# Differential attention in a fused decoder layer: k kept once per map with zeros, the scores as two products on all 128 channels

## The chip, the cores and the metric

The kernel runs on one core of a Trainium2 chip. The metric is the device time of one execution in microseconds (us), the median of the runs. A profile of one further execution shows what each engine did: TensorE (PE; its weight loads are shown apart as PEld), VectorE (DVE), ScalarE (ACT), GpSimd (POOL) and SyncE (SP), which issues most of the DMAs.

## The reference

One decoder layer over 256 tokens with 2048 channels: a projection, two token mixers side by side (gated DeltaNet and differential attention), gates, two further projections, a layer norm, a feed-forward part and a second layer norm. The change concerns the scores of the differential attention. It has 16 heads, each with two maps of 64 channels for q and k and 128 channels for v:

```python
def diff_attention(q, k, v, lam_params, norm_w, layer_idx):
    q = q.reshape(B, L, DA_HEADS, 2, DA_HEAD_DIM).transpose(0, 2, 3, 1, 4)
    k = k.reshape(B, L, DA_HEADS, 2, DA_HEAD_DIM).transpose(0, 2, 3, 1, 4)
    ...
    for blk in range(L // Q_BLOCK):
        start, end = blk * Q_BLOCK, (blk + 1) * Q_BLOCK
        ...
        bias = jnp.where(dist >= 0, -slopes[:, None, None] * dist, -jnp.inf)
        s = jnp.einsum('bhmqd,bhmkd->bhmqk', qb, kb).astype(jnp.float32) * scale + bias[None, :, None]
        p = jax.nn.softmax(s, axis=-1)
        p_diff = p[:, :, 0] - lam * p[:, :, 1]
        outs.append(jnp.einsum('bhqk,bhkd->bhqd', p_diff, vb.astype(jnp.float32)))
    ...
```

`Q_BLOCK` is 128, so a head has two blocks of queries: the first sees 128 keys, the second 256. With two maps that is 2 x 128 and 2 x 256 columns of scores.

## The kernel before

**The weight stream.** All weights pass through a ring of four tiles of 256 input channels by 512 output channels. SyncE loads a tile (`raw`), ScalarE rounds it (`whi`, its count is `hi_done`), VectorE takes the remainder (`wlo`, L1443, count `lo_done`), and TensorE multiplies it in `gemm_tile` with 12 products of 512 columns: two 128-channel halves, two halves of the tokens (`t`), and for each high x high, high x low and low x high. The activations are the stationary operand, the weights the moving one, the sums stand in the PSUM banks `pg`. ScalarE and VectorE work three tiles ahead of TensorE (`AHEAD`).

**Bodies and slots.** A `body` is 32 weight tiles, in four groups of eight; each tile is a slot `s` of 0 to 31. Every engine runs the same body, and at given slots it does a step of the token mixers besides its share of the weight stream. The order on each engine is the order in which the code is written; semaphores (`N[...]`) tie the engines together. After four bodies of the DeltaNet part comes a body that projects the first four heads' q, k and v of the attention (`N_DA`) and ends the DeltaNet part, then four bodies in each of which `da_mix` does the attention of four heads (`HB`), while the body's weights project the next four heads' q, k and v; the last of the four is `N_GB`.

**The attention of a head.** At slots 0, 5, 10 and 15 (`HEAD_SLOTS`) TensorE makes one head's scores, from `qT` (stationary) and `kT` (moving), both f32 with the channels on the partitions: map 0 is on partitions 0 to 63, map 1 on 64 to 127. For each block of queries `t` and each map `m` there is one product on 64 partitions, of 128 columns for `t` = 0 and 256 for `t` = 1; map 0 goes to bank `B[1]`, map 1 to `B[2]`. VectorE waits for `pe_s`, adds the ALiBi bias in one instruction for each map (384 columns), and takes the maxima; ScalarE makes the exponentials; VectorE normalizes and subtracts at `s0 + 2`; GpSimd moves p out to DRAM and back in pieces to transpose it (`turn_p`); at slots 10, 15, 20 and 25 (`PV_SLOTS`) TensorE multiplies p with v, three products of 128 columns on all 128 partitions.

**Where kT comes from.** For the first four heads VectorE transposes k in 16 blocks of 32 partitions in slots 16 to 23 of the body `N_DA` (`da_turns`, L1854). For the others ScalarE sends k through DRAM, and VectorE turns it in one instruction of 1024 elements a partition at slot 29 (`qk_rows`, L1840); q likewise at slot 21.

**Memory.** `act_b` takes the attention's result, high and low half, 16 heads of 256 tokens each. Until then its room holds the DeltaNet part's buffers (`cT`, `decm`, `T`, `Pm` and others).

Of the kernel before, what the change touches and what calls it, by code (L numbers as in the profile page):

```python
# [22 lines left out]
P = 128  # L23
# [5 lines left out]
HB = 4  # L29
# [75 lines left out]
def build(nc, xT, xrow, weights, w_ab, consts, early, params, lam_in, ln_in, out):  # L105
    ctx = ExitStack()

    def sb(name, shape, dt=F32):
        return ctx.enter_context(nc.sbuf_tensor(name, shape, dt))
# [4 lines left out]
    with ctx:  # L114
# [25 lines left out]
        stage = tmp("stage", [P, 4, 8, SB])  # L140
        oT = tmp("oT", [P, 4, 8, SB])
        dn.close()
        act_b = sb("act_b", [P, 2, KC, SEQ], F32R)
        gates = sb("gates", [P, 2, TOK, D])
        y = gates[:, 0]
# [40 lines left out]
        def c(name):  # L186
            a, b = CONST[name]
            return cst[:, a:b]
# [68 lines left out]
        def landed(buf):  # L257
            return flat(buf[:, :, :]).rearrange("p (a q x) -> p a q x", a=4, x=SB)

        def last_four(jj):  # L260
            return isinstance(jj, int) and jj == NB - 1

# [42 lines left out]
        def end_at(s):  # L305
# [25 lines left out]
        x_hi = sem("x_hi")  # L331
        x_lo = sem("x_lo")
        once = """pe_passed pe_ab pe_abT act_ab2 dve_ab2 act_abT dve_two pe_sc0 act_pro dve_pro dve_sc0 act_tot dve_lam act_lam
            dve_lnT dve_x1 pe_x1T x1f act_x1T dve_x1T pe_y act_beta act_gc pe_gT act_gT act_var dve_var act_root act_sig act_xn pro_chain ln_chain""".split()

        counted = """pe_conv dve_raw dve_conv act_silu dve_cw act_tap
            dve_g act_past act_decay pe_ktok act_sqk dve_ktail pe_kk dve_at dve_t act_tt dve_a8 pool_t8 dve_x pe_x pe_p dve_p pe_t
# [136 lines left out]
        def _(pe):  # L474
# [223 lines left out]
            def da_mix(j, s):  # L698
                for h, s0 in enumerate(HEAD_SLOTS):
                    if s == PV_SLOTS[h]:  # L700
                        pe.wait_ge(N["dve_pT"], 1 + HB * j + h + 1)
                        pe.wait_ge(N["dve_oh2"], 1 + HB * j + max(h - 1, 0))
                        pe.wait_ge(N["dve_oT"], 1 + 2 * NB)
                        o = B[3 if h % 2 == 0 else 0]
                        mm(o[:, 0:P], pT[:, 0:P], vda[:, 0, h * P:(h + 1) * P])
                        mm(o[:, P:2 * P], pT[:, P:2 * P], vda[:, 0, h * P:(h + 1) * P], True, False)
                        mm(o[:, P:2 * P], pT[:, 2 * P:3 * P], vda[:, 1, h * P:(h + 1) * P], False, True
                           ).then_inc(N["pe_pv"], 1)
                for h, s0 in enumerate(HEAD_SLOTS):
                    if s == s0:  # L710
                        pe.wait_ge(N["dve_qkT"], 1 + 2)
                        pe.wait_ge(N["dve_qkS"], 1 + 2 * j)
                        pe.wait_ge(N["dve_s1"], 1 + HB * j + h)
                        pe.wait_ge(N["dve_oT"], 1 + 2 * NB)
                        for t in range(TOK):
                            for m in range(2):
                                a = slice(m * CH, (m + 1) * CH)
                                last = mm(B[1 + m][:, t * P:t * P + (t + 1) * P],
                                          qT[a, h, t * P:(t + 1) * P], kT[a, h, 0:(t + 1) * P])
                        last.then_inc(N["pe_s"], 1)  # L720

            def turn_rows(cnt, n):
# [650 lines left out]
        def _(pool):  # L1373
# [23 lines left out]
            for j in range(NB + 1):  # L1397
                if j > 0:
                    pool.wait_ge(N["dve_qs"], 1 + j)
                    root(d_("rs"), d_("qs")).then_inc(N["pool_rs"], 1)  # L1400
                if j < NB:
                    pool.wait_ge(N["dve_ss"], 1 + j + 1)
                    ch(root(d_("rk"), d_("ss")))
                    G.tensor_tensor(d_("rinv"), d_("rk"), d_("ss"), ALU.mult).then_inc(N["pool_rinv"], 1)
                    pool.wait_ge(N["dve_a8"], 1 + j + 1)
                    for k in range(EB - 1):
                        col, row, part, rest = below(k)
                        ch(G.tensor_tensor(part, col, row, ALU.mult))  # L1408
                        last = G.tensor_tensor(rest, rest, part, ALU.subtract)  # L1409
                        if k < EB - 2:  # L1410
                            ch(last)
                    last.then_inc(N["pool_t8"], 1)
                    for i in range(2):
                        pool.wait_ge(c_kept, 16 * (2 * j + i + 1))
                        pool.wait_ge(N["dve_raw"], 1 + 2 * j + i)
                        blocks_in(turn_c, moved, c_full)
                    pool.wait_ge(v_kept, 16 * (j + 1))
                    blocks_in(turn_v, vtok, v_full)
            def os_root(i):

                pool.wait_ge(N["dve_os"], 1 + i + 1)
                root(sm[:, 48:50], sm[:, 42:44]).then_inc(N["pool_os"], 1)
# [16 lines left out]
        def _(dve):  # L1439
# [316 lines left out]
            def da_mix(j, s, ch):  # L1756
# [4 lines left out]
                for h, s0 in enumerate(HEAD_SLOTS):  # L1761
                    if s == s0:
                        dve.wait_ge(N["pe_s"], 1 + HB * j + h + 1)
                        dve.wait_ge(N["dve_pd"], 1 + HB * j + h)
                        for m in range(2):
                            ins = stt(pr[:, m, :], c("negdist"), sm[:, 44 + h:45 + h], B[1 + m][:, 0:3 * P],
                                      ALU.mult, ALU.add)
                        ins.then_inc(N["dve_s1"], 1)
                        dve.wait_ge(N["dve_s1"], 1 + HB * j + h + 1)
                        V.tensor_reduce(sm[:, 24:26], pr[:, :, 0:P], X, ALU.max)  # L1770
                        ch(V.tensor_reduce(sm[:, 26:28], pr[:, :, P:3 * P], X, ALU.max))
                        ts(sm[:, 28:32], sm[:, 24:28], -1.0, ALU.mult).then_inc(N["dve_mx"], 1)
# [61 lines left out]
            def qk_rows(j, s):  # L1834

                if s in DA_ROWS:
                    which = DA_ROWS.index(s)
                    dve.wait_ge(q_full, 64 * (2 * j + which - 1))
                    dve.wait_ge(N["pe_s"], 1 + HB * j)
                    V.transpose((qT, kT)[which][:, :, :].rearrange("p h (t a x) -> p a (h t) x", t=TOK, x=SB),  # L1840
                                gate_b(0).rearrange("p (a q i) -> p a q i", a=4, i=SB)).then_inc(N["dve_qkS"], 1)

            def da_turns(s):

                for which, slots in enumerate(DA_TURN_FIRST):
                    if s not in slots:
                        continue
                    at = sum(n for k, n in slots.items() if k < s)
                    if at == 0:
                        dve.wait_ge(evac[which], 2 * NB + 1)  # L1850
                    out = blocks_out((qT, kT)[which][:, :, :])
                    for i in range(at, at + slots[s]):
                        a, b = divmod(i, 4)
                        ins = V.transpose(out[b * SB:(b + 1) * SB, :, :, a, :], blocks_in[a * SB:(a + 1) * SB, :, :, b, :])  # L1854
                    if i == 15:
                        ins.then_inc(N["dve_qkT"], 1)
# [385 lines left out]
```

## Time and profile before

| | |
|---|---|
| time, median of 3 runs | 1903.24 us (1902.1 to 1903.43) |
| the profiled execution's own time | 1903.3 us |
| its span, first to last instruction | 1901.4 us |
| TensorE busy | 1885.8 us, 99% |
| VectorE busy | 1314.3 us, 69% |
| ScalarE busy | 918.5 us, 48% |
| GpSimd busy | 216.5 us, 11% |
| granted TensorE clock, mean | 0.998 |

The busy time of an engine is the union of its records. A record of TensorE lasts from its start until its last result is out, so records that follow each other overlap, and the starts, not the durations, show what one costs. An f32 product stands in the trace as two records, a product of the weight stream as one, though both are printed as f32. Idle time of an engine that isn't the bottleneck costs nothing.

### The profile page before, as it was taken

Reading aid. Unit: us, or ns where it says so; the run is one execution under the profiler, and the core shown is the slowest. Engines: PE = TensorE matmul, PEld = TensorE weight load, DVE = VectorE, ACT = ScalarE, POOL = GpSimd, SP = SyncE. Lnnn points to the kernel's source line nnn. Section 1 sums busy time; section 2 is a strip of 40 time slices with the busy share of each in tenths; the row PEclk is TensorE's granted clock in tenths of the full one; section 3 lists DMA queues with packets and bytes.
Section 4 is the critical chain, followed back from the end, with each engine's and each line's share of the span. In section 5 each row is a group of like instructions: output and inputs, shape, how many; then the busy total and the mean of one; then the engine's idle time right before and its main releaser. Section 6 shows DMA issues by size and latency. Waiting matters only on the chain.

```text
span 1901.4 us, 30042 instructions
## 1 busy us (share of the span) xinstructions
PE 1885.8 (99%) x9703; PEld 1554.5 (82%) x9703; DVE 1314.3 (69%) x1816; ACT 918.5 (48%) x1270; POOL 216.5 (11%) x480
## 2 busy tenths in 40 slices
PE   9999999999999999999999999999999999999997
PEld 7888888878888888888888887888888888888886
DVE  7878788787766767676577657667775466655656
ACT  5656565554454545456444437444443444443442
POOL 0303031131024232323000000000000000000000
PEclk9999999999999999999999999999999999999999
DMA  7666657574557676766656675555656556655555
GB/s 271 209 193 211 211 190 222 173 241 155 194 190 244 213 248 206 247 211 210 209 189 198 222 248 173 194 193 190 196 192 196 190 191 197 197 191 196 189 190 175
DMA packets 115091, 387.61 MB, mean 204 GB/s; under 512 B 14193, under 2 KB 21169, under 8 KB 114865
## 3 DMA queue, kind: packets, MB, share of 16 engines
q1 hardware_dynamic: 97904, 351.65, 56.5%
q10 hardware_dynamic: 11712, 22.04, 3.6%
q0 software_dynamic: 5376, 12.59, 2.4%
q8 instruction: 64, 1.05, 0.2%
q14 instruction: 35, 0.28, 0.1%
HBM read 367.86 MB, written 18.37 MB: 203 GB/s over the span
## 4 chain that ended last, share of the span: by engine, by line
PE 92%; DVE 3%; issue 1%; POOL 1%; DMA 1%; ACT 1%; SPq 0%; DVEq 0%; ACTq 0%; POOLq 0%
PE pg L476 87%; PE B L476 4%; DVE gates L1451 1%; DVE cT L1451 1%; POOL Tc L1408 1%; DMA qT<-turn_c 1%; ACT whi L854 1%; DVE wlo L1443 0%; DMA raw<-in_weights 0%; POOL Tc L1409 0%; POOL qT L1394 0%; PE B L576 0%; PE B L595 0%; PE B L689 0%; DVE Pm L1443 0%
## 5 line engine op out<-in xcount | busy, mean ns | idle before, releaser
L1443 DVE TENSOR_TENSOR wlo<-raw,whi 128x1024 fp32r<-128x1024 f32 (+1 forms) x640 | 778.9, 1219 | 470.2 <-ACT whi L854 452.8
L854 ACT ACTIVATE whi<-raw 128x1024 fp32r<-128x1024 f32 (+1 forms) x640 | 673.7, 1057 | 731.9 <-PE pg L476 712.5
L476 PE MATMUL pg<-whi,act_x 128*128 128x512 f32 x2960 | 938.6, 393 | 1.7 <-ACT whi L854 1.7
L476 PEld LDWEIGHTS pg<-whi,act_x 128*128 128x128 f32 x2960 | 555.5, 188 | 124.8 <-issue 7.9
L476 PE MATMUL pg<-wlo,act_x 128*128 128x512 f32 x1480 | 574.5, 389 | 0.0
L476 PE MATMUL pg<-whi,act_a 128*128 128x512 f32 x1632 | 504.8, 389 | 0.2 <-DVE act_a L1443 0.2
L476 PEld LDWEIGHTS pg<-whi,act_a 128*128 128x128 f32 x1632 | 306.3, 188 | 64.3 <-DVE act_a L1443 0.8
L476 PEld LDWEIGHTS pg<-wlo,act_x 128*128 128x128 f32 x1480 | 278.1, 188 | 54.6
L476 PE MATMUL pg<-wlo,act_a 128*128 128x512 f32 x816 | 317.4, 389 | 0.0
L476 PEld LDWEIGHTS pg<-wlo,act_a 128*128 128x128 f32 x816 | 153.2, 188 | 31.7
L476 PE MATMUL pg<-whi,act_b 128*128 128x512 f32 x512 | 158.5, 389 | 0.0
L476 PEld LDWEIGHTS pg<-whi,act_b 128*128 128x128 f32 x512 | 96.1, 188 | 20.0
L476 PE MATMUL pg<-wlo,act_b 128*128 128x512 f32 x256 | 99.6, 389 | 0.0
L1884 DVE STREAM_TRANSPOSE soft<-hraw 32x256 f32<-32x256 f32 x208 | 90.6, 436 | 3.8
L476 PEld LDWEIGHTS pg<-wlo,act_b 128*128 128x128 f32 x256 | 48.0, 188 | 10.0
L1383 POOL TENSOR_TENSOR half<-dsm 128x8 f32<-128x8 f32 x24 | 13.2, 550 | 264.9 <-DVE dsm L1448 263.6
L1451 DVE SCALAR_TENSOR_TENSOR cT<-vda,cw,cT 128x255 f32<-128x255 f32 (+2 forms) x96 | 41.9, 478 | 1.1
L1156 ACT ACTIVATE soft<-soft,sm 128x128 f32<-128x128 f32 (+1 forms) x64 | 28.4, 445 | 27.8 <-DVE sm L1447 27.7
L1385 POOL TENSOR_SCALAR half<-half 128x2 f32<-128x2 f32 (+1 forms) x72 | 32.2, 448 | 6.3
L1451 DVE SCALAR_TENSOR_TENSOR soft<-cst,sm,B 128x384 f32<-128x384 f32 x32 | 18.2, 611 | 21.0 <-PE B L476 20.3
L1394 POOL DMA_DIRECT2D gates<-turn_p x48 | 26.2, 552 | 38.2 <-DMA turn_p<-gates 38.2
L993 ACT ACTIVATE cT<-cT 128x1024 f32<-128x1024 f32 x12 | 12.7, 1062 | 23.6 <-DVE cT L1451 23.6
(259 smaller groups left out, 1100.5 us busy)
## 6 DMA issues: line engine op xcount, KB each, us to landing
raw<-in_weights SPq DMA_DIRECT2D x646, 512.0 KB, 4.2
turn_c<-hraw ACTq DMA_DIRECT2D x8, 512.0 KB, 3.9
qT<-turn_c POOLq DMA_DIRECT2D x32, 128.0 KB, 3.2
turn_q<-hraw ACTq DMA_DIRECT2D x6, 512.0 KB, 3.8
gates<-turn_q ACTq DMA_DIRECT2D x24, 128.0 KB, 4.8
turn_p<-gates POOLq DMA_DIRECT2D x12, 192.0 KB, 3.7
gates<-turn_p POOLq DMA_DIRECT2D x48, 48.0 KB, 3.9
decm<-sums_out ACTq DMA_DIRECT2D x4, 512.0 KB, 3.7
```

The source lines that it names most:

```text
L476: return nc.tensor.matmul(o, l, r, start=start, stop=stop)
L854: return nc.scalar.activation(o, i, ACT.Copy, scale=scale)
L993: nc.scalar.activation(cT[:, kind], cT[:, kind], ACT.Silu).then_inc(N["act_silu"], 1)
L1156: last = nc.scalar.activation(pr[:, m, a:b], pr[:, m, a:b], ACT.Exp, bias=sm[:, 28 + i:29 + i], accum_out=sm[:, 32 + i:33 + i])
L1383: ch(G.tensor_tensor(a, o, o, ALU.mult))
L1385: ch(G.tensor_scalar(a, a, -0.5, 1.5, ALU.mult, ALU.add))
L1394: pool.dma_start(dst[b * SB:(b + 1) * SB], scratch[:, :, b].rearrange("a x (q i) -> x a q i", i=SB)).then_inc(full, 16)
L1408: ch(G.tensor_tensor(part, col, row, ALU.mult))
L1443: return V.tensor_tensor(o, a, b, op)
L1451: return V.scalar_tensor_tensor(out=o, in0=a, scalar=s, in1=b, op0=op0, op1=op1)
L1884: ins = V.transpose(blocks_out(turned)[b * SB:(b + 1) * SB, :, :, a, :], blocks_in[a * SB:(a + 1) * SB, :, :, b, :])
```

## The change

- k is no longer kept in `kT` but in `k_span`, once for each map: map 0's copy has its own 64 channels on partitions 0 to 63 and zeros on 64 to 127, map 1's the other way round. Product and sum over all 128 partitions then give one map's scores, since the other map's channels of q meet zeros.
- `k_span` lies in the part of `act_b` that belongs to the last four heads' results, which are written after the last scores; its two halves are 4096 elements apart.
- GpSimd writes the zeros once, after its last work for the DeltaNet part and ahead of the first move of p; TensorE waits for that (`pool_zero`) in front of each head's scores.
- A head's scores are two products, one for each block of queries: the moving operand is map 0's and map 1's keys, one behind the other, 256 columns for `t` = 0 into `B[1]` and 512 for `t` = 1 into `B[2]`.
- VectorE adds the bias in one instruction for each block of queries (256 and 512 columns).
- `qk_rows` turns k in two instructions of 64 partitions, `da_turns` writes its 16 blocks to the map that they belong to.

```diff
--- before.py
+++ after.py
@@ -140,6 +140,10 @@
         stage = tmp("stage", [P, 4, 8, SB])
         oT = tmp("oT", [P, 4, 8, SB])
         dn.close()
+        da = ExitStack()
+        da.enter_context(nc.sbuf_tensor("da_below", [P, (KC - HB) * SEQ], F32))
+        k_span = da.enter_context(nc.sbuf_tensor("k_span", [P, 2, KC * SEQ], F32))
+        da.close()
         act_b = sb("act_b", [P, 2, KC, SEQ], F32R)
         gates = sb("gates", [P, 2, TOK, D])
         y = gates[:, 0]
@@ -257,6 +261,12 @@
         def landed(buf):
             return flat(buf[:, :, :]).rearrange("p (a q x) -> p a q x", a=4, x=SB)
 
+        k_maps = [k_span[:, m, 0:HB * SEQ].rearrange("p (h s) -> p h s", h=HB) for m in range(2)]
+        MAPS = [slice(0, CH), slice(CH, P)]
+
+        def both_maps(h, n):
+            return k_span[:, :, h * SEQ:h * SEQ + n]
+
         def last_four(jj):
             return isinstance(jj, int) and jj == NB - 1
 
@@ -331,7 +341,7 @@
         x_hi = sem("x_hi")
         x_lo = sem("x_lo")
         once = """pe_passed pe_ab pe_abT act_ab2 dve_ab2 act_abT dve_two pe_sc0 act_pro dve_pro dve_sc0 act_tot dve_lam act_lam
-            dve_lnT dve_x1 pe_x1T x1f act_x1T dve_x1T pe_y act_beta act_gc pe_gT act_gT act_var dve_var act_root act_sig act_xn pro_chain ln_chain""".split()
+            dve_lnT pool_zero dve_x1 pe_x1T x1f act_x1T dve_x1T pe_y act_beta act_gc pe_gT act_gT act_var dve_var act_root act_sig act_xn pro_chain ln_chain""".split()
 
         counted = """pe_conv dve_raw dve_conv act_silu dve_cw act_tap
             dve_g act_past act_decay pe_ktok act_sqk dve_ktail pe_kk dve_at dve_t act_tt dve_a8 pool_t8 dve_x pe_x pe_p dve_p pe_t
@@ -712,11 +722,11 @@
                         pe.wait_ge(N["dve_qkS"], 1 + 2 * j)
                         pe.wait_ge(N["dve_s1"], 1 + HB * j + h)
                         pe.wait_ge(N["dve_oT"], 1 + 2 * NB)
+                        pe.wait_ge(N["pool_zero"], 1)
                         for t in range(TOK):
-                            for m in range(2):
-                                a = slice(m * CH, (m + 1) * CH)
-                                last = mm(B[1 + m][:, t * P:t * P + (t + 1) * P],
-                                          qT[a, h, t * P:(t + 1) * P], kT[a, h, 0:(t + 1) * P])
+                            n = (t + 1) * P
+                            last = mm(B[1 + t][:, 0:2 * n].rearrange("p (m s) -> p m s", m=2),
+                                      qT[:, h, t * P:(t + 1) * P], both_maps(h, n))
                         last.then_inc(N["pe_s"], 1)
 
             def turn_rows(cnt, n):
@@ -1416,6 +1426,13 @@
                         blocks_in(turn_c, moved, c_full)
                     pool.wait_ge(v_kept, 16 * (j + 1))
                     blocks_in(turn_v, vtok, v_full)
+            pool.wait_ge(N["act_x21"], 1 + NB)
+            pool.wait_ge(N["dve_qk"], 1 + 2 * NB)
+            pool.wait_ge(N["pool_rs"], 1 + NB)
+            ch(G.memset(k_maps[0][MAPS[1]], 0.0))
+            G.memset(k_maps[1][MAPS[0]], 0.0).then_inc(N["pool_zero"], 1)
+            pool.wait_ge(N["pool_zero"], 1)
+
             def os_root(i):
 
                 pool.wait_ge(N["dve_os"], 1 + i + 1)
@@ -1762,9 +1779,9 @@
                     if s == s0:
                         dve.wait_ge(N["pe_s"], 1 + HB * j + h + 1)
                         dve.wait_ge(N["dve_pd"], 1 + HB * j + h)
-                        for m in range(2):
-                            ins = stt(pr[:, m, :], c("negdist"), sm[:, 44 + h:45 + h], B[1 + m][:, 0:3 * P],
-                                      ALU.mult, ALU.add)
+                        for t, (a, b) in enumerate([(0, P), (P, 3 * P)]):
+                            ins = stt(pr[:, :, a:b], rep(c("negdist")[:, a:b], 2), sm[:, 44 + h:45 + h],
+                                      B[1 + t][:, 0:2 * (b - a)].rearrange("p (m s) -> p m s", m=2), ALU.mult, ALU.add)
                         ins.then_inc(N["dve_s1"], 1)
                         dve.wait_ge(N["dve_s1"], 1 + HB * j + h + 1)
                         V.tensor_reduce(sm[:, 24:26], pr[:, :, 0:P], X, ALU.max)
@@ -1837,8 +1854,16 @@
                     which = DA_ROWS.index(s)
                     dve.wait_ge(q_full, 64 * (2 * j + which - 1))
                     dve.wait_ge(N["pe_s"], 1 + HB * j)
-                    V.transpose((qT, kT)[which][:, :, :].rearrange("p h (t a x) -> p a (h t) x", t=TOK, x=SB),
-                                gate_b(0).rearrange("p (a q i) -> p a q i", a=4, i=SB)).then_inc(N["dve_qkS"], 1)
+                    rows = gate_b(0).rearrange("p (a q i) -> p a q i", a=4, i=SB)
+
+                    def by_token(dst):
+                        return dst.rearrange("p h (t a x) -> p a (h t) x", t=TOK, x=SB)
+                    if which == 0:
+                        last = V.transpose(by_token(qT[:, :, :]), rows)
+                    else:
+                        for m in range(2):
+                            last = V.transpose(by_token(k_maps[m][MAPS[m]]), rows[MAPS[m]])
+                    last.then_inc(N["dve_qkS"], 1)
 
             def da_turns(s):
 
@@ -1848,9 +1873,9 @@
                     at = sum(n for k, n in slots.items() if k < s)
                     if at == 0:
                         dve.wait_ge(evac[which], 2 * NB + 1)
-                    out = blocks_out((qT, kT)[which][:, :, :])
                     for i in range(at, at + slots[s]):
                         a, b = divmod(i, 4)
+                        out = blocks_out(qT[:, :, :] if which == 0 else k_maps[b // 2])
                         ins = V.transpose(out[b * SB:(b + 1) * SB, :, :, a, :], blocks_in[a * SB:(a + 1) * SB, :, :, b, :])
                     if i == 15:
                         ins.then_inc(N["dve_qkT"], 1)
```

TensorE's order in the second body of the attention, at the slot where p times v of the first head is followed by the third head's scores: `B1` and `B2` are the banks of the scores, `B3` that of p times v, `pg` those of the weight stream. Before:

```order
L476 MATMUL pg11<-wlo,act_x 128x512
L476 MATMUL pg11<-whi,act_x 128x512
L476 MATMUL B3<-vda,soft 128x128 x3
L713 REGISTER_ALU
L476 MATMUL B1<-kT,qT 128x128
L476 MATMUL B2<-kT,qT 128x128
L476 MATMUL B1<-kT,qT 128x256
L476 MATMUL B2<-kT,qT 128x256
L501 REGISTER_ALU
L476 MATMUL pg10<-whi,act_x 128x512
```

After:

```order
L486 MATMUL pg11<-wlo,act_x 128x512
L486 MATMUL pg11<-whi,act_x 128x512
L486 MATMUL B3<-vda,soft 128x128 x3
L723 REGISTER_ALU
L486 MATMUL B1<-k_span,qT 128x256
L486 MATMUL B2<-k_span,qT 128x512
L511 REGISTER_ALU
L486 MATMUL pg10<-whi,act_x 128x512
```

Nothing moved past anything; the four products of the scores are two, at the same place.

VectorE's order from the k turn at slot 29 of the first body of the attention to the scores' bias in the next one (`wlo` is the weight split, `sm` holds slopes and maxima). Before:

```order
L1451 SCALAR_TENSOR_TENSOR gates<-gates,par 128x256
L1840 STREAM_TRANSPOSE kT<-gates 128x4x8x32
L1443 TENSOR_TENSOR wlo<-raw,whi 128x1024 x2
...
L1759 COPY sm<-cst 128x4
L357 ISA
L1763 REGISTER_ALU
L1451 SCALAR_TENSOR_TENSOR soft<-cst,sm,B 128x384 x2
L1770 TENSOR_REDUCE sm<-soft 128x2
```

After:

```order
L1468 SCALAR_TENSOR_TENSOR gates<-gates,par 128x256
L1865 STREAM_TRANSPOSE k_span<-gates 64x4x8x32 x2
L1460 TENSOR_TENSOR wlo<-raw,whi 128x1024 x2
...
L1776 COPY sm<-cst 128x4
L367 ISA
L1780 REGISTER_ALU
L1468 SCALAR_TENSOR_TENSOR soft<-cst,sm,B 128x2x128
L1468 SCALAR_TENSOR_TENSOR soft<-cst,sm,B 128x2x256
L1787 TENSOR_REDUCE sm<-soft 128x2
```

One transpose of k became two of half the partitions, ahead of the next weight split; the two instructions of the bias have other shapes.

## Rows read from the trace of the kernel before

**Rows 1.** The page, busy us of each engine (share of the span) xinstructions.
```profile
PE 1885.8 (99%) x9703; PEld 1554.5 (82%) x9703; DVE 1314.3 (69%) x1816; ACT 918.5 (48%) x1270; POOL 216.5 (11%) x480
...
PEclk9999999999999999999999999999999999999999
```

**Rows 2.** TensorE's waits, the largest: waited for, us in all, times, longest.
```profile
PE pg L476 <- ACT whi L854: 1.7, 3, 0.9
```

**Rows 3.** TensorE's timeline: start us, us from first start to last end, instruction xcount.
```profile
530.12 0.39 PE L476 MATMUL pg<-whi,act_x 128*128 128x512 f32 x1
530.44 0.93 PE L476 MATMUL B<-kT,qT 64*128 64x128 f32 x8
531.29 0.50 PE L476 MATMUL pg<-whi,act_x 128*128 128x512 f32 x1
...
543.22 0.39 PE L476 MATMUL pg<-wlo,act_x 128*128 128x512 f32 x1
...
543.90 0.39 PE L476 MATMUL pg<-wlo,act_x 128*128 128x512 f32 x1
...
544.81 0.39 PE L476 MATMUL pg<-whi,act_x 128*128 128x512 f32 x1
...
559.49 0.40 PE L476 MATMUL pg<-whi,act_x 128*128 128x512 f32 x1
...
574.83 0.40 PE L476 MATMUL pg<-whi,act_x 128*128 128x512 f32 x1
...
590.16 0.40 PE L476 MATMUL pg<-whi,act_x 128*128 128x512 f32 x1
590.39 0.83 PE L476 MATMUL B<-vda,soft 128*128 128x128 f32 x6
...
604.48 0.40 PE L476 MATMUL pg<-whi,act_x 128*128 128x512 f32 x1
...
636.43 0.39 PE L476 MATMUL pg<-whi,act_x 128*128 128x512 f32 x1
```

**Rows 4.** The same timeline in four narrow windows inside the first score block.
```profile
530.44 0.38 PE L476 MATMUL B<-kT,qT 64*128 64x128 f32 x2
...
530.65 0.50 PE L476 MATMUL B<-kT,qT 64*128 64x128 f32 x4
...
530.76 0.39 PE L476 MATMUL B<-kT,qT 64*128 64x256 f32 x2
...
530.98 0.38 PE L476 MATMUL B<-kT,qT 64*128 64x256 f32 x2
```

**Rows 5.** Groups by form, 480 to 900 us: xcount | busy us, mean ns | idle before.
```profile
L476 PE MATMUL B<-vda,soft 128*128 128x128 f32 x96 | 13.3, 275 | 0.0
L476 PEld LDWEIGHTS B<-vda,soft 128*128 128x128 f32 x96 | 13.2, 191 | 1.3
```

**Rows 6.** The same view, VectorE's bias step.
```profile
L1451 DVE SCALAR_TENSOR_TENSOR soft<-cst,sm,B 128x384 f32<-128x384 f32 x32 | 18.2, 611 | 21.0 <-PE B L476 20.3 <-DVE sm L1759 0.7
```

**Rows 7.** VectorE's timeline, at a k turn and behind a bias step; idle time in brackets.
```profile
616.87 1.24 DVE L1840 STREAM_TRANSPOSE kT<-gates 128x1024 f32<-128x1024 f32 x1
618.04 1.18 DVE L1443 TENSOR_TENSOR wlo<-raw,whi 128x1024 fp32r<-128x1024 f32 x1
620.38 1.23 DVE L1443 TENSOR_TENSOR wlo<-raw,whi 128x1024 fp32r<-128x1024 f32 x1 [1.16 <-ACT whi L854]
...
632.11 1.23 DVE L1443 TENSOR_TENSOR wlo<-raw,whi 128x1024 fp32r<-128x1024 f32 x1 [1.73 <-ACT whi L854]
```

**Rows 8.** GpSimd's timeline, the first move of p.
```profile
540.13 0.61 POOL L1429 DMA_DIRECT2D turn_p<-gates  x1 [68.37 <-DVE gates L1451]
```

**Rows 9.** Timelines of TensorE and its weight loads, the warm-up products at the start.
```profile
3.34 1.06 PE L476 MATMUL B<-TTf 128*128 128x512 f32 x1
...
4.19 1.06 PE L476 MATMUL B<-TTf 128*128 128x512 f32 x1
...
3.34 0.34 PEld L476 LDWEIGHTS B<-TTf 128*128 128x128 f32 x1 [0.52 <-issue]
```

## The prediction

> **What bounds the kernel now.** I read the busy shares first: TensorE is busy in 1885.8 of 1901.4 us [rows 1]. Then the view of who waited for whom, for TensorE: its largest entry is 1.7 us, for ScalarE's rounding of the weights [rows 2]. So no other engine holds TensorE anywhere for long, and a change in the length of TensorE's own work goes to the end one to one, as long as what feeds it keeps its lead. The attention scores are TensorE's work. What a block of them costs has to be read as time added between two weight products, because a record's own duration contains its run through the array and overlaps its neighbour's.
>
> **What the score block costs now.** The timeline of TensorE gives the last weight product ahead of slots 0, 5, 10, 15, 20 and 25 of a body: 530.12, 544.81, 559.49, 574.83, 590.16 and 604.48 [rows 3]. Between two of them stand five weight tiles, 60 products, and what the attention puts in. The step of a weight product is (543.90 - 543.22)/3 = 0.2267 us [rows 3], so 60 take 13.60. What is left is
> - slots 0 and 5, scores alone: 14.69 - 13.60 = 1.09 and 14.68 - 13.60 = 1.08, mean 1.085;
> - slots 10 and 15, a p·v block and then scores: 15.34 and 15.33, so 1.74 and 1.73, mean 1.735;
> - slot 20 (and 25), p·v alone: 14.32 - 13.60 = 0.72.
> There are four such bodies, so 8 score blocks stand alone and 8 behind a p·v.
>
> Inside a block [rows 4]: an f32 product is two records, one for each pass over its columns. The eight records start in four pairs, at 530.44, 530.65, 530.76 and 530.98: map 0 on channels 0 to 63 and map 1 on channels 64 to 127 start together and stream side by side. So the two maps' 128 + 256 columns cost once: the columns of a pair step 0.11 (128) and 0.22 (256). Four pairs of columns are 2 x 0.107 + 2 x 0.213 = 0.64 us. The other 0.445 us of 1.085 is the changeover: the first record starts 0.32 behind the weight product instead of 0.23, the second pair 0.21 behind the first where 128 columns need 0.11 (its weights weren't loaded ahead), and the weight product comes back at 531.29, 0.31 behind the last pair's start where 256 columns need 0.21 [rows 3, 4]; the rest is the first weight products behind the block, which load late.
>
> The Trainium skill's "TensorEngine Tiling (Array Packing)", section Key Properties, states both halves: tiles work independently, and changing the tiling mode drains the engine. The trace agrees with both, with the pairs and with the 0.09 and 0.10 us at the two ends. The second half speaks for this change: taken alone it would make the kernel 16 x 0.19 = 3.0 us faster; the first half speaks against it, and by the rows it is the larger.
>
> **What it costs after.** The order of the changed program shows on TensorE, in place of four products on 64 channels, two on all 128: one of 256 columns into bank 1 and one of 512 into bank 2. With 128 channels in use nothing streams beside them. Records: 2 of 256 and 2 of 512 columns.
> - Price of a pass. The p·v block is the nearest row: whole-array f32 products back to back. Its six records take 0.83 in the timeline, the last of them 0.275 [rows 3, 5], so the step is (0.83 - 0.275)/5 = 0.111 for 128 columns, which is 0.1067 (two cycles a column at 2.4 GHz; the granted clock is at 9 tenths or more in every slice [rows 1]) and 0.005. Low end: columns alone, 12 x 0.1067 = 1.28. Taken: 1.28 and 0.005 for each of four records, 1.30. High end: the step of weight products, 0.2267 where 512 single columns are 0.2133, is 6% over its columns; so 1.36. I take 1.30, because p·v is the same data type in the same mode.
> - Price of the way in and out. p·v alone adds 0.72, of which 6 x 0.1116 = 0.67 are steps; 0.05 stay for coming and going without a change of mode.
> - Scores alone: 1.30 + 0.05 = 1.35 against 1.085, +0.265, 8 times: 2.12 us.
> - Scores behind p·v: 0.67 + 1.30 + 0.05 = 2.02 against 1.735, +0.285, 8 times: 2.28 us.
> - Sum +4.40 us. With the low end 8 x 0.245 + 8 x 0.265 = 4.08, with the high end 8 x 0.325 + 8 x 0.345 = 5.36.
>
> **The parts beside it.**
> - VectorE's bias step: two instructions of 384 elements, 0.611 each [rows 6], become one of 256 and one of 512, the same 768 elements; the nearest is no change. It starts 0.27 later. The smallest lead I found for weights is behind such a step: the split that starts at 632.11 and takes 1.23 feeds the tile that starts at 636.43 [rows 3, 7], so 3.09 us are left. 0.27 fit. Cost 0; uncovered, 0.27 per head.
> - The k turn between bodies: one transpose of 1024 elements, 1.24 [rows 7], becomes two on 64 partitions each. Since the elements of a partition set the time, I take +1.24, three times (bodies 2 to 4). It pushes the split behind it from 618.04 to 619.28, its end to 620.5; the next split stood idle 1.16 until 620.38 [rows 7]. So it is taken up within a slot. Below nothing it can't go, for the elements don't shrink. The first body's 16 block transposes are the same number as before.
> - GpSimd's zeroing: two fills of 64 x 1024, once. No fill of that size stands in the trace. GpSimd is idle for 68.37 us before 540.13, so from 471.77 on [rows 8]; what is queued behind the fills is the first move of p at 540.13, and TensorE asks at 530.4. Anything from nothing to 58.6 us for the two fills is hidden; at 60 us it would cost 1.4. I take 0. The waits ahead of the fills are for steps of the DeltaNet part, which are over by then.
> - TensorE's new wait is for a semaphore that rises once, long before; its sequencer runs ahead of the array as it does at p·v, where the weights are loaded under the product before. Queued behind it are the scores and all later weight tiles. Cost 0.
>
> Span 1901.4 + 4.4 = 1905.8. The profiled execution's own time is 1903.3, 1.9 over its span and 0.06 over the median, so the same sum is made on the median: 1903.24 + 4.40 = **1907.6 us**.
>
> **Rivals.**
> - A, faster: an f32 pass over whole columns is as cheap as a weight product's. The rows tempt to it, both are printed 128x512 f32, and the weight product steps 0.2267. Then the scores take 2 x 0.113 + 2 x 0.227 = 0.68; alone 0.73 (-0.355), behind p·v 1.40 (-0.335): -5.5 us, 1897.7. It decides from a 512-column step of 0.34 downwards (3 steps of that are 1.30 - 0.275). Against it: p·v, 0.111 for 128 columns, and the pair of 256 at 0.22. Chance 0.04.
> - B, smaller loss: part of a record's step is a fixed price, so that half as many, longer records save. If 0.025 of p·v's 0.1116 were fixed, 256 columns would take 0.198 and 512 0.371: 1.14 in all, alone +0.105, behind p·v +0.125, +1.8 us, 1905.1. Against it: 0.11 and 0.22 for 128 and 256 leave nothing fixed [rows 4]. The Trainium skill's tiling page, section Instruction Overhead, speaks of about 60 cycles for each matmul on trn2, which is the 0.025 at 2.4 GHz; the trace doesn't agree, with 0.005. Chance 0.05.
> - C, larger loss: the 512-column pass is slow. The only whole-array f32 passes of 512 in the trace step 0.85 (3.34 to 4.19) [rows 9]. Then 2 x 0.42 more per head, 13.4 us, 1921.1. Against it: weight loads there take 0.34, and 0.19 at p·v [rows 5, 9], so this stretch ran at the lower clock level, though it stands ahead of the first clock record. For it: the moving operand is now in two pieces far apart, and no row has such a product. Chance 0.03.
> - D: VectorE loses its lead and the three turns come through: 3.7 us more, 1911.3. Chance 0.03.
>
> **How the numbers follow.** The forecast has 0.85. About 0.2% of this kernel, 3.8 us, is what a measurement can tell from no change, and the forecast lies just beyond it: its bounds are 4.1 to 5.4, while the shown runs of the kernel before lie between 1.14 below and 0.19 above their median. So 0.13 of the 0.85 goes to "same". Slower: 0.72 + C + D = 0.78. Same: 0.13 + B = 0.18. Faster: A, 0.04. Range: 1903.24 + 4.08 - 1.14 = 1906.2 to 1903.24 + 5.36 + 0.67 (half the spread of the runs) = 1909.3; that leaves out the four rivals, 0.15 in all.
>
> **What would show it.** In the profile after: four records of the scores per head, steps of 0.22 (256 columns) and 0.43 (512); the first one 0.23 behind the weight product, not 0.32; the weight product right behind the last; 14.95 us between the weight products ahead of slots 0 and 5, and 15.62 for slots 10 and 15, each in place of 14.69 and 15.33; TensorE's waits as small as before. I am wrong if the 512-column step is far from 0.43 (A, B, C), if TensorE waits for VectorE's splits (D), or if the way in still costs a changeover, which would add up to 0.4 us per head.

## The result: 0.22% slower, and the profile after

The changed kernel takes 1907.16 us (median of 17 runs, 1906.08 to 1909.21), the kernel before in the same comparison 1902.45 us (17 runs, 1901.8 to 1903.84). The ratio is 1.0022, with a 95% interval of 1.0015 to 1.0029: 4.7 us more, and between 2.9 and 5.5 by the interval. The forecast was +4.4 us. The profiled span is 1905.2 us.

The page of the changed kernel, engine busy times (the line that answers to [rows 1]), and the largest waits of TensorE (that of [rows 2]; who waited for whom: us in total, times, longest):

```profile
PE 1889.6 (99%) x9639; PEld 1558.3 (82%) x9639; DVE 1317.3 (69%) x1819; ACT 918.3 (48%) x1270; POOL 217.3 (11%) x482
```

```profile
PE B L486 <- DVE TTf L1490: 1.5, 1, 1.5
PE pg L486 <- ACT whi L864: 1.4, 2, 0.8
```

The first of them stands in the view of the kernel before as well, just below the line of [rows 2]:

```profile
PE B L476 <- DVE TTf L1473: 1.5, 1, 1.5
```

TensorE has 3.8 us more to do and 64 records less, four for each head. Nothing new holds it: no entry names VectorE's weight splits (`wlo`), GpSimd or the zeroing, and from 529 to 890 us, over the attention's four bodies, the view of TensorE's waits is empty in both kernels. VectorE has 3.0 us more: the three k turns are 3.7 us longer, and a little went elsewhere.

TensorE's timeline of the changed kernel at the first scores and at the last weight product ahead of slots 0, 5, 10, 15, 20 and of the next body's slot 0 (start, us from the first start to the last end, instruction, count):

```profile
529.65 0.40 PE L486 MATMUL pg<-whi,act_x 128*128 128x512 f32 x1
529.88 1.46 PE L486 MATMUL B<-k_span,qT 128*128 128x256 f32 x4
530.78 0.79 PE L486 MATMUL pg<-whi,act_x 128*128 128x512 f32 x1
531.41 0.40 PE L486 MATMUL pg<-wlo,act_x 128*128 128x512 f32 x1
...
544.59 0.40 PE L486 MATMUL pg<-whi,act_x 128*128 128x512 f32 x1
...
559.53 0.40 PE L486 MATMUL pg<-whi,act_x 128*128 128x512 f32 x1
...
575.11 0.40 PE L486 MATMUL pg<-whi,act_x 128*128 128x512 f32 x1
...
590.69 0.40 PE L486 MATMUL pg<-whi,act_x 128*128 128x512 f32 x1
...
624.77 0.40 PE L486 MATMUL pg<-whi,act_x 128*128 128x512 f32 x1
```

Against [rows 3]: 14.94 us twice in place of 14.69 and 14.68, 15.58 twice in place of 15.34 and 15.33. So a head's scores cost 0.25 us more, alone and behind p·v alike, and the way from slot 0 to the next body's slot 0 is 95.12 us. In the kernel before it is 94.12 (530.12 to the row below), so 1.00 us a body and 4.0 us for the four bodies:

```profile
624.24 0.39 PE L476 MATMUL pg<-whi,act_x 128*128 128x512 f32 x1
```

The difference of the two profiled spans is 3.8; the 0.2 that are missing lie outside the attention: the changed kernel came to slot 0 at 529.65 and not at 530.12, 0.5 earlier, in a part that the change doesn't touch, and lost 0.3 again behind the attention.

The same timeline in three narrow windows inside the first block, for the steps ([rows 4] of before):

```profile
530.11 0.81 PE L486 MATMUL B<-k_span,qT 128*128 128x256 f32 x2
...
530.32 1.02 PE L486 MATMUL B<-k_span,qT 128*128 128x512 f32 x2
...
530.75 0.59 PE L486 MATMUL B<-k_span,qT 128*128 128x512 f32 x1
```

With 529.88 for the first record the starts are 529.88, 530.11, 530.32 and 530.75: 0.44 for the two records of 256 columns, so 0.22 each, and 0.43 for the first of 512. The first record stands 0.23 behind the weight product, where it was 0.32. The record of the weight product that follows starts at 530.78, only 0.03 behind the last one, but that start is not its price: the record after it comes at 531.41, 0.66 behind 530.75, which is the 0.43 of the last scores and one weight step of 0.23. There is no changeover left, and no two records of the scores start together.

### The profile page after: what moved, and what is told of

It reads as the page before. It is cut to its first block, busy times and chain, and to the rows that moved or that the text cites. A ratio compares the mean times of both kernels' runs of the same rounds, so it can differ in the third digit from the quotient of the medians.

```text
span 1905.2 us, 29921 instructions
## 1 busy us (share of the span) xinstructions
PE 1889.6 (99%) x9639; PEld 1558.3 (82%) x9639; DVE 1317.3 (69%) x1819; ACT 918.3 (48%) x1270; POOL 217.3 (11%) x482
## 4 chain that ended last, share of the span: by engine, by line
PE 95%; DVE 2%; issue 1%; ACT 1%; DMA 1%; POOL 0%; SPq 0%; DVEq 0%; ACTq 0%; POOLq 0%
PE pg L486 90%; PE B L486 5%; DVE gates L1468 1%; DMA raw<-in_weights 0%; ACT whi L864 0%; DMA qT<-turn_c 0%; DVE wlo L1460 0%; DVE cT L1468 0%; POOL Tc L1418 0%; PE B L586 0%; PE B L699 0%; PE B L605 0%; POOL Tc L1419 0%; DVE act_b L1460 0%; ACT gates L1287 0%
## 5 line engine op out<-in xcount | busy, mean ns | idle before, releaser
L1468 DVE SCALAR_TENSOR_TENSOR soft<-cst,sm,B 128x256 f32<-128x256 f32 (+1 forms) x32 | 18.2, 611 | 26.6 <-PE B L486 25.4
```

The lines of the kernel that those rows point to most:

```text
L1468: return V.scalar_tensor_tensor(out=o, in0=a, scalar=s, in1=b, op0=op0, op1=op1)
```

## The experiments

All are compared by the same two places of TensorE's timeline: the last weight product ahead of slot 0, and the one ahead of slot 5 (or of slot 0 in the next body). From 528 to 890 us no run shows a wait of TensorE, so the time between two such places depends on TensorE's own work alone.

### What stands around the products: x1_kept

The changed kernel with the old products on the new storage:

```diff
                         for t in range(TOK):
-                            n = (t + 1) * P
-                            last = mm(B[1 + t][:, 0:2 * n].rearrange("p (m s) -> p m s", m=2),
-                                      qT[:, h, t * P:(t + 1) * P], both_maps(h, n))
+                            for m in range(2):
+                                a = slice(m * CH, (m + 1) * CH)
+                                last = mm(B[1 + m][:, t * P:t * P + (t + 1) * P],
+                                          qT[a, h, t * P:(t + 1) * P], k_maps[m][a, h, 0:(t + 1) * P])
...
-                        for t, (a, b) in enumerate([(0, P), (P, 3 * P)]):
-                            ins = stt(pr[:, :, a:b], rep(c("negdist")[:, a:b], 2), sm[:, 44 + h:45 + h],
-                                      B[1 + t][:, 0:2 * (b - a)].rearrange("p (m s) -> p m s", m=2), ALU.mult, ALU.add)
+                        for m in range(2):
+                            ins = stt(pr[:, m, :], c("negdist"), sm[:, 44 + h:45 + h], B[1 + m][:, 0:3 * P],
+                                      ALU.mult, ALU.add)
```

> The changed kernel with its scores put back: k stays kept once per map with the zeros, the two-part k turn, GpSimd's zeroing and TensorE's wait for it stay, but the scores are again four products on 64 partitions with a bank for each map, and the bias is added per map. My theory (the loss is TensorE's columns, which no longer run two maps side by side): the score blocks cost what they did, 14.69 and 15.33 us between the weight products ahead of slots 0 and 5 and of slots 10 and 15, and the time is that of the kernel before, within 0.2 us in the span. Rival (the loss comes from what stands around the products: the longer k turn, the zeroing, the wait): the time stays near the changed kernel's, 3.8 us over the kernel before.

Measured: 1903.48 us against 1902.94, ratio 1.0003 (0.9994 to 1.0012), span 1900.3. TensorE's timeline, ahead of slots 0 and 5 and of the next body's slot 0:

```profile
528.75 0.39 PE L486 MATMUL pg<-whi,act_x 128*128 128x512 f32 x1
...
543.44 0.39 PE L486 MATMUL pg<-whi,act_x 128*128 128x512 f32 x1
...
622.87 0.39 PE L486 MATMUL pg<-whi,act_x 128*128 128x512 f32 x1
```

14.69 and 94.12 us, as in the kernel before. So storage, zeros, k turn and the new wait cost nothing, and the whole 1.00 us a body is in the form of the products and of the bias step, which this run puts back too. (The bias step's new form stays in x4_one_map_128 below, where TensorE waits for nothing either.) The span is 1.1 less than the kernel before's and not within 0.2 as expected; the difference arises ahead of the attention, 528.75 against 530.12. A comparison of single spans of this kernel is good to about that much, while the stretch between two places comes out alike in all four bodies.

### The pairing: x3_one_map_64, x6_same_rows, x2_map_major

Three edits of the kernel before. In the first, map 1 is left out:

```diff
-                            for m in range(2):
+                            for m in range(1):
...
-                            ins = stt(pr[:, m, :], c("negdist"), sm[:, 44 + h:45 + h], B[1 + m][:, 0:3 * P],
+                            ins = stt(pr[:, m, :], c("negdist"), sm[:, 44 + h:45 + h], B[1][:, 0:3 * P],
```

> The kernel before with map 1's score products left out (two products a head on 64 partitions; VectorE reads map 0's scores for both maps, so the second map is not computed). Theory: map 1 ran under map 0, so leaving out half of the score work gives back almost nothing on TensorE: 14.65 to 14.69 us between the weight products ahead of slots 0 and 5, time within 0.5 us of the kernel before. Rival (every record pays its own columns): half of the columns gone is 0.32 us a head or more, at least 5 us less.

Measured: 1902.81 us, ratio 0.9997 (0.9988 to 1.0006). Its score block, and the way to slot 5:

```profile
528.74 0.39 PE L476 MATMUL pg<-whi,act_x 128*128 128x512 f32 x1
529.05 0.92 PE L476 MATMUL B<-kT,qT 64*128 64x128 f32 x4
529.90 0.50 PE L476 MATMUL pg<-whi,act_x 128*128 128x512 f32 x1
...
543.42 0.39 PE L476 MATMUL pg<-whi,act_x 128*128 128x512 f32 x1
```

Four records where there were eight, and 14.68 us where there were 14.69. In the kernel before, map 1 costs TensorE next to nothing.

In the second, both maps' products are put on partitions 0 to 63; map 1's own channels are left out, and map 0's are used twice:

```diff
-                                a = slice(m * CH, (m + 1) * CH)
+                                a = slice(0, CH)
```

> The kernel before with map 1's products made from map 0's channels, so that all four products of a head are on partitions 0 to 63 (map 1 is not computed from its own channels, its scores are those of map 0). Still two changeovers, but no second group of rows to stream beside. The exchanged loops didn't separate the maps, since the records of the two halves paired up again; this does. Theory: the columns add up, 1.28 us in place of 0.64: +0.64 for each of 16 heads, +10.2 us over the kernel before, so the mode with 64 channels is by itself slower than the changed kernel (by 5.5 to 6 us) and owes its lead to the pairing alone. Rival (64 channels are quicker for another reason than the pairing): less than 5 us over the kernel before.

Measured: 1912.65 us, ratio 1.0054 (1.0041 to 1.0068), span 1910.7, so +10.3 us by the ratio.

```profile
529.21 0.39 PE L476 MATMUL pg<-whi,act_x 128*128 128x512 f32 x1
529.53 1.57 PE L476 MATMUL B<-kT,qT 64*128 64x128 f32 x8
531.03 0.50 PE L476 MATMUL pg<-whi,act_x 128*128 128x512 f32 x1
...
544.54 0.39 PE L476 MATMUL pg<-whi,act_x 128*128 128x512 f32 x1
```

The same eight records now last 1.57 and not 0.93 [rows 3], the way is 15.33: +0.64 a head, which is the 0.64 us of columns that ran beside the others. The smaller products owe their lead over the changed kernel to the pairing alone; one after the other on 64 partitions they are 0.39 us a head slower than it.

The third was meant to separate the maps in another way, by order:

```diff
-                        for t in range(TOK):
-                            for m in range(2):
+                        for m in range(2):
+                            for t in range(TOK):
```

> The kernel before with the two loops around its four score products exchanged: both blocks of queries of map 0 first, then both of map 1, same products, same partitions, same banks. In the kernel before the partner of each record on the other 64 partitions stands next to it; here only the last record of map 0 and the first of map 1 are neighbours. Theory: the array keeps the order of records, so only that pair overlaps: columns 0.107 + 0.107 + 0.213 + 0.213 + 0.213 + 0.213 = 1.07 us a head in place of 0.64, so +0.43 for 16 heads, +6.9 us over the kernel before and about 3 us over the changed one, since both changeovers stay as well. Rival (the near-simultaneous starts are only how the records look and the two maps do not run side by side): no difference, 0 us.

Measured: 1902.8 us, ratio 0.9999 (0.999 to 1.0008). Neither theory as I had written it: the time is the rival's, and the rival's reason is refuted by the two runs above. The order of the program as it was built is map 0's two products, then map 1's:

```
L476 MATMUL B1<-kT,qT 128x128
L476 MATMUL B1<-kT,qT 128x256
L476 MATMUL B2<-kT,qT 128x128
L476 MATMUL B2<-kT,qT 128x256
```

and TensorE's timeline in narrow windows inside the block is

```profile
529.00 0.39 PE L476 MATMUL B<-kT,qT 64*128 64x128 f32 x2
...
529.22 0.50 PE L476 MATMUL B<-kT,qT 64*128 64x128 f32 x4
...
529.33 0.39 PE L476 MATMUL B<-kT,qT 64*128 64x256 f32 x2
...
529.55 0.39 PE L476 MATMUL B<-kT,qT 64*128 64x256 f32 x2
```

Two records of 128 columns start together at 529.00, two at 529.22 (the line there counts the next pair in, x4), two of 256 columns at 529.33 and two at 529.55. In the program map 0's 256-column records stand ahead of all of map 1's, yet all four records of 128 columns, map 1's two among them, start ahead of any record of 256. The trace doesn't say which record of a pair is whose. As x6_same_rows shows that records on the same rows don't share their time, each pair must be one record of each map; so each half of the rows works through its own records, and the halves don't wait for each other. Loops exchanged or not, the pairs form again.

### The changeover: x4_one_map_128, x5_two_heads

The changed kernel with map 0 alone, so with as long a stream of columns as the pairs of the kernel before, but on the whole array:

```diff
-                            last = mm(B[1 + t][:, 0:2 * n].rearrange("p (m s) -> p m s", m=2),
-                                      qT[:, h, t * P:(t + 1) * P], both_maps(h, n))
+                            last = mm(B[1 + t][:, 0:n], qT[:, h, t * P:(t + 1) * P], k_maps[0][:, h, 0:n])
...
-                                      B[1 + t][:, 0:2 * (b - a)].rearrange("p (m s) -> p m s", m=2), ALU.mult, ALU.add)
+                                      rep(B[1 + t][:, 0:b - a], 2), ALU.mult, ALU.add)
```

> The changed kernel with only map 0's scores: two products on all 128 partitions of 128 and 256 columns, VectorE reads them for both maps, so the second map is not computed. It has the same length of columns in time as the pairs of the kernel before (0.64 us a head), but no change of mode, so it prices the changeover. Theory: per head 0.64 + 0.02 + 0.05 = 0.71 alone and 1.34 with p times v in front of it, against 1.085 and 1.735: -0.375 x 8 - 0.395 x 8 = -6.2 us against the kernel before, and 0.64 x 16 = 10.2 us less than the changed kernel. Rival (a record has a large fixed price, or the 512-column form is what is slow): against the changed kernel clearly less than 10.2 us is saved, or clearly more.

Measured: 1897.4 us, ratio 0.9971 (0.996 to 0.9982), span 1895.0.

```profile
528.99 0.40 PE L486 MATMUL pg<-whi,act_x 128*128 128x512 f32 x1
529.22 0.82 PE L486 MATMUL B<-k_span,qT 128*128 128x128 f32 x4
529.69 0.58 PE L486 MATMUL pg<-whi,act_x 128*128 128x512 f32 x1
...
543.29 0.40 PE L486 MATMUL pg<-whi,act_x 128*128 128x512 f32 x1
...
621.59 0.40 PE L486 MATMUL pg<-whi,act_x 128*128 128x512 f32 x1
```

14.30 us to slot 5, so 0.70 for the block, and 92.60 for the body: 1.52 less than the kernel before, 0.38 a head. That is what going to 64 rows and back costs. Against the changed kernel it is 2.52 a body, 0.63 a head: the columns of the second map. The change is the sum of the two: -0.38 and +0.63, +0.25. For the four bodies the two are 6.1 and 10.1 us, where 6.2 and 10.2 were expected.

Where the 0.38 lies shows in the starts. This run's second and last record and the second weight product behind the block:

```profile
529.33 0.49 PE L486 MATMUL B<-k_span,qT 128*128 128x128 f32 x2
...
529.66 0.38 PE L486 MATMUL B<-k_span,qT 128*128 128x256 f32 x1
...
530.11 0.40 PE L486 MATMUL pg<-wlo,act_x 128*128 128x512 f32 x1
```

and that weight product in the kernel before:

```profile
531.63 0.39 PE L476 MATMUL pg<-wlo,act_x 128*128 128x512 f32 x1
```

On the way in the second record starts 0.34 behind the weight product ahead of the block (529.33 - 528.99); in the kernel before the second pair starts 0.53 behind it (530.65 - 530.12 [rows 3, 4]). On the way out the second weight product starts 0.45 behind the last record here and 0.65 behind the last pair there (531.63 - 530.98). That is 0.19 and 0.20. The first record behind each change of mode shows only half of that (0.09 and 0.10, as the prediction has it), the second one the rest. The weight loads go with it: in the kernel before they begin together with the products that they are for, behind a gap, at 530.44 and at 531.29:

```profile
530.44 0.52 PEld L476 LDWEIGHTS B<-kT,qT 64*128 64x128 f32 x8 [0.35 <-issue]
531.29 0.19 PEld L476 LDWEIGHTS pg<-whi,act_x 128*128 128x128 f32 x1 [0.33 <-issue]
```

In the changed kernel the first load of the scores runs under the weight product that starts at 529.65, 0.23 ahead of its own product:

```profile
529.65 0.85 PEld L486 LDWEIGHTS B<-k_span,qT 128*128 128x128 f32 x4
```

If a block costs 0.38 us for the changeover, heads in one block should share it. The kernel before with the second head's scores moved to slot 0:

```diff
+SCORE_SLOTS = [0, 0, 10, 15]
...
+        def score_bank(h, m):
+            return B[3 * m] if h == 1 else B[1 + m]
...
-                for h, s0 in enumerate(HEAD_SLOTS):
+                for h, s0 in enumerate(SCORE_SLOTS):
                     if s == s0:
+                        if h == 1:
+                            pe.wait_ge(N["dve_oh2"], 1 + HB * j)
...
-                        pe.wait_ge(N["dve_s1"], 1 + HB * j + h)
+                        pe.wait_ge(N["dve_s1"], 1 + HB * j + (h if h > 1 else 0))
```

with `score_bank(h, m)` for `B[1 + m]` in the products and in the bias step.

> The kernel before with the scores of the first two heads of a body made in one block at slot 0 (the second head's into the two banks of p times v, which are free then), instead of at slots 0 and 5; VectorE takes the second head at slot 5 as before. The products are the same, but a body has one changeover less. Theory (a changeover in and out costs about 0.42 us a block, columns 0.64): 4 x 0.42 = 1.7 us less than the kernel before, so about 1901.2 us and 5.5 us less than the changed kernel. Rival (what a block costs beyond its columns belongs to each head or record, not to the change of mode): no change.

Measured: 1901.05 us, ratio 0.9991 (0.9982 to 1.0).

```profile
529.33 0.39 PE L480 MATMUL pg<-whi,act_x 128*128 128x512 f32 x1
529.65 1.58 PE L480 MATMUL B<-kT,qT 64*128 64x128 f32 x16
...
558.26 0.40 PE L480 MATMUL pg<-whi,act_x 128*128 128x512 f32 x1
...
623.01 0.39 PE L480 MATMUL pg<-whi,act_x 128*128 128x512 f32 x1
```

Sixteen records take 1.58 where eight take 0.93: the second head adds 0.65, its columns and next to nothing. The body is 93.68 us, 0.44 less than before, 1.76 for the four. That is more than x4's 0.38, because a block less also saves the 0.06 that x4's block costs over its columns (0.70 - 0.64) without any change of mode. The interval of the times only just reaches no change; the timeline is clear.

### Two changeovers less: x7_two_pairs

The same for both pairs of heads. The banks have room: a head takes 384 of 512 columns in `B[1]` and `B[2]`, p·v 256 in `B[0]` and `B[3]`. The second head of a pair goes into what is left:

```diff
-HEAD_SLOTS = [0, 5, 10, 15]
+HEAD_SLOTS = [0, 5, 10, 14]
+SCORE_SLOTS = [0, 0, 10, 10]
...
+        def score_at(h, m, a, b):
+            if h % 2 == 0:
+                return B[1 + m][:, a:b]
+            if b <= P:
+                return B[1 + m][:, 3 * P + a:3 * P + b]
+            return B[3 * m][:, P + a:P + b]
```

TensorE makes the scores ahead of p·v at slot 10, its later p·v wait for the fourth head's bias step, and VectorE waits for both heads of a pair.

> As the run with two heads in one block at slot 0, and the third and fourth head also in one block, at slot 10 ahead of the first p times v: the second head of a pair goes into the columns of the four banks that are otherwise unused, and the fourth head's bias step moves from slot 15 to slot 14. Two changeovers less in each body. Theory: 8 x 0.42 = 3.4 us less than the kernel before, about 1899.6 us; a few tenths may go to p times v standing alone at slot 15. If TensorE has to wait for the fourth head's bias step at slot 15, the gain is smaller and shows as a wait for VectorE. Rival (no price for the changeover): no change.

Measured: 1899.59 us against 1902.84, ratio 0.9985 (0.9976 to 0.9994), span 1898.3.

```profile
530.64 0.39 PE L484 MATMUL pg<-whi,act_x 128*128 128x512 f32 x1
...
559.89 1.58 PE L484 MATMUL B<-kT,qT 64*128 64x128 f32 x16
...
623.99 0.39 PE L484 MATMUL pg<-whi,act_x 128*128 128x512 f32 x1
```

The body is 93.35 us (530.64 to 623.99), 0.77 less than before and 1.77 less than in the changed kernel: 3.1 us for the four bodies, where 3.4 were expected. Part of what is missing is that p·v at slot 15 no longer shares its way in and out with scores; no run takes that apart. It is faster than the kernel before with an interval that leaves out no change, and faster than the changed kernel by 7.1 us of the bodies.

## Why the prediction was right

- **The bound.** TensorE's own work goes to the end one to one: +4.0 us in the attention's bodies, +4.7 in the medians with an interval of 2.9 to 5.5. How near the number came is in part luck. The bodies' 4.0 lie just under the low end of the forecast's sum, 4.08, and the 0.7 more that the medians show is within their interval and has no cause that a run shows. The sum also started from 1903.24, the median of three runs, which is 0.8 above that of the 17; so the time came out 0.4 below the forecast although the measured change is 0.3 above it.
- **What the block cost.** 0.64 of columns for two maps and the rest changeover. Shown: taking map 1 away changes 0.01 us of 14.69, putting it on the same rows adds 0.64.
- **The changeover's size.** The 0.19 us that I read at the two ends (0.09 and 0.10) are half of it. The other half is that weights are not loaded ahead, which shows at the second pair and behind the first weight product. x4 gives 0.38 for the whole, 0.19 on the way in and 0.20 on the way out. The 0.445 that the prediction calls the changeover holds 0.06 more, which a block costs without a change of mode too; x5, with one block less, saves all of it, 0.44. The sum was right because it went by whole blocks, 1.085 and 1.735, and didn't add up the parts. The 16 x 0.19 = 3.0 us that the prediction puts down to the change of mode, taken alone, would be 16 x 0.38 = 6.1; it is too small by half, but no term of the sum.
- **The price of a pass.** Steps of 0.22 and 0.43, as forecast. The term that was sized too high is the block behind p·v: 15.58 - 13.60 = 1.98 measured, 2.02 forecast; alone 1.34 and 1.35. Both blocks come out 0.06 above their columns (1.34 - 1.28 and 1.98 - 1.92), where the forecast had 0.07 and 0.10: the 0.005 us for each record and 0.05 for coming and going, both from p·v, don't add up over a longer block. That is the 0.4 us between 4.4 and 4.0.
- **The work beside it.** VectorE's k turn:

```profile
617.41 2.49 DVE L1865 STREAM_TRANSPOSE k_span<-gates 64x1024 f32<-64x1024 f32 x2
619.92 2.36 DVE L1460 TENSOR_TENSOR wlo<-raw,whi 128x1024 fp32r<-128x1024 f32 x2
```

  Two of 1.24, and the two splits behind them back to back; in [rows 7] the second stood idle for 1.16 first. That gap took up the delay, as forecast, and x1_kept shows no cost. GpSimd's zeroing:

```profile
471.42 0.96 POOL L1432 MEMSET k_span<- 64x1024 f32 x1
472.44 0.95 POOL L1433 MEMSET k_span<- 64x1024 f32 x1
```

  1.9 us, over 56 us before it is asked for.
- **The bias step's start.** This was forecast too small. It was to come 0.27 us later, the whole difference of the blocks; measured from the last weight product ahead of slot 0 it starts at 1.80 (531.45 - 529.65) and not at 1.36 (531.48 - 530.12), 0.44 later:

```profile
531.48 1.14 DVE L1451 SCALAR_TENSOR_TENSOR soft<-cst,sm,B 128x384 f32<-128x384 f32 x2 [0.29 <-DVE sm L1759]
```

```profile
531.45 1.14 DVE L1468 SCALAR_TENSOR_TENSOR soft<-cst,sm,B 128x256 f32<-128x256 f32 x2 [0.72 <-DVE sm L1776]
```

  VectorE waits for the last of the scores. The added columns stand ahead of that, while half of the changeover that went away stood behind it. The lead of 3.09 us took this up as well, and the step itself is as long as it was.
- **The rivals.** A (a long pass as cheap as a weight product's) and C (a slow one, or two pieces far apart that cost something) would have shown in the step of 0.43; neither did. B asked for 0.37 at 512 columns and 0.20 at 256; there are 0.43 and 0.22. D would have shown as a wait of TensorE for the splits; there is none.
- **The chance of "same"** was not idle: an effect of 4.0 us stands close to what the runs can resolve, and only the ratio over 17 runs of each, together with the steps, makes it certain.

## What to carry to other kernels

Two products that each fill half of the array's rows cost as much as one here, if they sit on different rows; joining them over zeros makes the array do the zeros' work and doubles the columns' time. Going to such a mode and back costs about 0.4 us a block here, so the thing to save is the number of blocks: put more products in each, rather than give up the pairing. And price a block by the time between two neighbours of the stream around it: durations of overlapping records show neither the pairing nor the changeover.

## What the runs showed of the hardware that I had not expected

The two halves of the rows don't keep the program's order between them. In x2_map_major all of map 0's records stand ahead of map 1's, yet the timeline shows four pairs, 529.00, 529.22, 529.33 and 529.55, and the 14.70 us on the way to slot 5 would be about 15.12 by the expectation's sum, an estimate, had the records started in the program's order (the body is 622.83 - 528.68 = 94.15 us, 0.03 over the kernel before):

```profile
528.68 0.39 PE L476 MATMUL pg<-whi,act_x 128*128 128x512 f32 x1
...
543.38 0.39 PE L476 MATMUL pg<-whi,act_x 128*128 128x512 f32 x1
...
622.83 0.39 PE L476 MATMUL pg<-whi,act_x 128*128 128x512 f32 x1
```

The Trainium skill's "TensorE: Matmul & The Clock Gate", section The mechanism (of its part on packing small matmuls), says that matmuls start and end strictly in program order, and that only weight loads are pulled ahead. The trace doesn't agree for products on different rows, and it decides here: the start times are out of the program's order. Map 1's records of 128 columns start ahead of both of map 0's of 256, and with one record of each map in a pair, three of map 1's four start ahead of map 0's last one. The four pairs and the unchanged 14.70 us say the same; how far one half may run ahead was not tried.
